# A transformer kernel on one Trainium2 core: the first product behind the turned features waits per eighth, with fewer warm-up products

## The chip, the core and the metric

The kernel runs on one core of one Trainium2 chip. The metric is device time in microseconds of one execution, from the first to the last instruction with what lies around them; the number for a kernel is the median of its runs. All data are float32. Engines are named as in the profile: PE is TensorE (its matmuls; PEld are its weight loads), DVE is VectorE, ACT is ScalarE, POOL is GpSimd, SP is SyncE, which issues the DMAs.

## The reference

Two blocks of two layers each work on 256 tokens of 1024 features. The change lies in the first block. Cut to what matters:

```python
for l in range(DEPTH):                                   # 2 layers
    shift1, scale1, gate1, shift2, scale2, gate2 = split(cond @ w_ada[l] + b_ada[l])
    h = x * (1 + scale1) + shift1
    y = token_mixer(h, w_in[l], ...)                     # p = h @ w_in; attention, spatial gating, gates
    x = layer_norm(ALPHA * x + gate1 * y, ...)
    h = x * (1 + scale2) + shift2
    y = moe_ffn(h, router_w[l], ...)                     # scores = sigmoid(h @ router_w); 64 experts, top 8
    x = layer_norm(ALPHA * x + gate2 * y, ...)
```

So each mixer and each expert layer begins in the same way: x, which lies with the tokens on the partitions, is turned so that features lie on the partitions, is modulated by scale and shift (one pair for each feature, so one for each partition once x is turned), and is then multiplied by a weight matrix: w_in in the mixer, router_w in the expert layer. The second block (attention, a recurrent mixer, two MLPs) is not touched.

## The kernel before

All five engines run one long program each, written out by hand, with semaphores between them. An engine's steps run in program order. `at[...]` holds for each named step the semaphore and the count at which it is done; `reach(pe, ...)` (L329) makes TensorE wait for one, unless it has already waited for as much of the same semaphore. VectorE's steps all count up one semaphore, ScalarE's another.

**The turning.** `turned_pe` (L561) turns x in two halves of 128 tokens (t = 0, 1). Each half is eight transposes of 128x128 (L578), into four PSUM banks; bank k2 holds the eighths 2*k2 and 2*k2 + 1, an eighth being 128 features by 256 tokens. The first half is turned as soon as the layer norm has written it, the second when its turn comes. Around the halves `keep_warm` (L301, products recorded under L304) issues products of the identity whose result nobody reads; they fill TensorE's idle time. After the second half there are six of them (L582), except in the mixer of layer 0, where six stand after the sums of the modulations instead (L944). In the profile each float32 product is two records, so six products are 12.

**The modulation.** `turned_out` (L584) writes the eighths from PSUM into SBUF with scale and shift, one instruction for each eighth. VectorE takes 0, 1, 4 and 5 (recorded under L171), ScalarE takes 2, 3, 6 and 7 (L145). They run beside the warm-up products.

**The wait.** `turned_done` (L594) makes TensorE wait for the last eighth of each engine, 5 and 7, so for all eight. It stands before the first product in `mixer_pe` (L945) and in `moe_pe` (L1499). A `group` (L225) is eight products, one for each eighth, summed in one PSUM bank in the order 0 to 7.

**What follows in a mixer.** `mixer_pe` (L946) multiplies by 15 tiles of w_in, two groups to a tile. Tiles 0 to 6 give two groups of 128 tokens each (i is the tile, t the token half); VectorE copies the results of tiles 0 to 2 out, ScalarE those of 3 to 6. Between them TensorE sums up partial modulations of later steps (`sums_of_partial_pe`, L368, recorded under L376 and L381) that VectorE has formed from pieces of w_ada (`partial_dve`, L356, recorded under L171 and L166). w_in and w_ada come through one DMA queue of SyncE, `mixer_sp` (L904), in turn one tile of w_in and two pieces of w_ada; a transfer into a tile is issued when its former content has been used. VectorE goes on to the rope of queries and keys once the modulations up to tile 7 are made (L1089). POOL loads the mixer's tables at its start (`mixer_pool`, L885).

**What follows in an expert layer.** `moe_pe` (L1497) forms the scores of the router: two groups of eight products, 128 tokens each, 64 columns wide (L1503). Then come the gate product of the shared expert and three warm-up products (L1520). The rest waits for the routing, which VectorE makes (`moe_dve`, L1799). On VectorE the order is: the eighths, then the low part of x less its rounded copy (L1806, recorded under L162), for which ScalarE must have made that copy, and only then the first step on the scores (L1814, recorded under L162 too). On ScalarE (`moe_act`, L1723) the order is: its eighths, the rounded copy of the first half (L1731), the sigmoid of the scores (L1733), the copy of the second half. With the routing of the first four experts made, TensorE gathers their tokens (`gather`, L1552, recorded under L229).

Of the kernel before, what the change touches and what calls it, by code (L numbers as in the profile page):

```python
# [224 lines left out]
def group(pe, out, pairs, start=True, stop=True):  # L225

    ins = None
    for i, (a, b) in enumerate(pairs):
        ins = pe.matmul(out, a, b, start=start and i == 0, stop=stop and i == len(pairs) - 1)  # L229
    return ins  # L230

def program(nc, D, out):
    ctx = ExitStack()
    with ctx:
# [3 lines left out]
        at = Values()  # L239
# [33 lines left out]
        made = signal("pe_made")  # L273
# [27 lines left out]
        def keep_warm(pe, b, n):  # L301

            for _ in range(n):
                pe.matmul(b[:, 0:256], ident[:, :], condr[:, 0:256], start=True, stop=True)  # L304
# [24 lines left out]
        def reach(pe, sem, n):  # L329

            if reached.get(sem, 0) < n:
                pe.wait_ge(sem, n)
                reached[sem] = n
# [227 lines left out]
        def turned_pe(pe, l, which, ready):  # L561

            xk = XS[:, :].rearrange("p (t d k) -> p t k d", t=2, k=8)
            for k2 in range(4):
                _, old = psum.take(("turned", l, which, k2), ("turned out", l, which, 2 * k2 + 1))
                freed(pe, old)
            if l or which:
                keep_warm(pe, psum.of["turned", l, which, 0], 7 if which else 14)
                spare, old = psum.take(("turned warm", l, which))
                freed(pe, old)  # L570
            for t in range(2):
                if t and (l or which):
                    keep_warm(pe, spare, 2 if which else 5)
                reach(pe, *at[ready(t)])
                for k2 in range(4):
                    for kk in range(2):
                        c = kk * 256 + t * 128
                        ins = pe.transpose(psum.of["turned", l, which, k2][:, c:c + 128], xk[:, t, 2 * k2 + kk, :], ident[:, :])  # L578
                    if t:
                        ins.then_inc(*made(("turned", l, which, k2)))  # L580
            if l or which:
                keep_warm(pe, spare, 6)  # L582

        def turned_out(eng, do, mine, dst, l, which):  # L584
            o = l * 32 + which * 16
# [5 lines left out]
                do.fma(dst[:, k * 256:k * 256 + 256], psum.of["turned", l, which, k // 2][:, k % 2 * 256:k % 2 * 256 + 256],  # L591
                       mod1[:, o + 8 + k:o + 9 + k], mod1[:, o + k:o + k + 1], ("turned out", l, which, k))

        def turned_done(eng, l, which):  # L594
            eng.wait_ge(*at["turned out", l, which, 5])
            eng.wait_ge(*at["turned out", l, which, 7])

        LN = [small[:, 16:40].rearrange("p (t s c) -> p t s c", t=2, s=2), small[:, 48:52].rearrange("p (t c) -> p t c", t=2),
              small[:, 52:54]]
# [276 lines left out]
        M = MixerMemory()  # L876
# [49 lines left out]
        def mixer_pe(pe, pump, l):  # L926
            reach(pe, *at["ident"])
            if l == 0:
                reach(pe, *at["cond rows"])
                b, old = psum.take("warm", "cond rows")  # L930
# [5 lines left out]
            if l == 0:  # L936
                sums_of_partial_pe(pe, 0)
                for n in range(4 * FROM[0] - 2, 4 * FROM[0]):
                    reach(pe, *at["mod piece", n])
                    keep_warm(pe, b, 4)  # L940
                sums_of_partial_pe(pe, 1)
                b, old = psum.take("warm behind")
                freed(pe, old)
                keep_warm(pe, b, 6)  # L944
            turned_done(pe, l, 0)  # L945
            for i in range(7):  # L946
                w = weights.of["w_in", l, i].rearrange("p (k c) -> p k c", k=8)
                reach(pe, *at["w_in", l, i])
                for t in range(2):
                    b, old = psum.take(("pz", l, i, t), ("pz out", l, i, t))  # L950
                    freed(pe, old)
                    group(pe, b[:, 0:256], [(M.hv[:, k, t * 128:t * 128 + 128], w[:, k, :]) for k in range(8)]) \
                        .then_inc(*made(("pz", l, i, t)))
                    if t == 0:
                        for u in vector_at(l, i):
                            sums_of_partial_pe(pe, u)
            for i in range(7, 15):
                w = weights.of["w_in", l, i].rearrange("p (k c) -> p k c", k=8)
                reach(pe, *at["w_in", l, i])
                for c in range(2):  # L960
                    b, old = psum.take(("gates", l, i, c), ("gates out", l, i, c))
# [7 lines left out]
            for a in range(3):  # L969
                b, old = psum.take(("qkT", l, a), ("qkT out", l, a))  # L970
                freed(pe, old)
                for s in range(2):
                    for t in range(2):
# [4 lines left out]
                        ins = pe.transpose(b[:, s * 256 + t * 128:s * 256 + t * 128 + 128], src, ident[:, :])  # L978
# [7 lines left out]
            for gg in range(2):  # L986
                b, old = psum.take(("sgu", l, gg), ("sgu out", l, gg))
                freed(pe, old)
                for g in range(4 * gg, 4 * gg + 4):
                    o = g % 4 * 128  # L990
                    ins = pe.matmul(b[:, o:o + 128].rearrange("p (t d) -> p t d", t=2), M.wsv[:, g, :],
                                    M.Zv[:, :, 512 + g * 64:576 + g * 64], start=True, stop=True)
# [184 lines left out]
        E = ExpertMemory()  # L1177
# [318 lines left out]

        def moe_pe(pe, l):  # L1497
            turned_pe(pe, l, 1, lambda t: ("ln", ("mixer", l), t))
            turned_done(pe, l, 1)  # L1499
            reach(pe, *at["router", l])  # L1500
            b, old = psum.hold(ACC, ("scores", l), ("scores out", l))
            freed(pe, old)
            for t in range(2):  # L1503
                ins = group(pe, b[:, t * 64:t * 64 + 64],
                            [(E.hv[:, k, t * 128:t * 128 + 128], E.rv[:, k, :]) for k in range(8)])
            ins.then_inc(*made(("scores", l)))
            def shared_half(name):
                b, w = psum.of[name, l], weights.of["ws_" + name[7:], l].rearrange("p (k f) -> p k f", k=8)
                reach(pe, *at["ws_" + name[7:], l])
# [2732 lines left out]
```

## Time and profile before

| | |
|---|---|
| median of 3 runs | 2992.61 us (2990.23 to 2993.92) |
| profiled execution, its own time | 2994.28 us |
| its span, first to last instruction | 2992.5 us |
| mean granted TensorE clock | 0.984 |
| PE busy | 2798.5 us, 94% of the span |
| DVE busy | 1629.0 us, 54% |
| ACT busy | 756.6 us, 25% |
| HBM traffic | 239 GB/s over the span |
| the two mixers of the first block begin to turn at | 21.5 us and 805.8 us |
| the two expert layers begin to turn at | 259.5 us and 1023.1 us |

Times in the profile count from the span's start. The profiled execution took 1.78 us more than its span. A timeline row reads: start, duration, engine, line, operation, names written<-read, shape, number of instructions merged in it, and in brackets the idle time of the engine ahead of it with what ended it. A row of stretches reads: the stretch, its length, for each engine its busy time and instructions, the granted TensorE clock as a share of full speed, the busy share of the 16 DMA engines, and GB/s. A row of grouped instructions ends with busy time, mean ns of one, and idle time ahead of them.

### The profile page before, as it was taken

The page shows a single profiled execution, that of the slowest core. Times are in us where ns is not written, and L with a number is a line of the kernel's source. Part 1 is how long each engine was busy: PE and PEld are TensorE (multiplying, and loading weights), DVE is VectorE, ACT ScalarE, POOL GpSimd, SP SyncE. Part 2 cuts the span into 40 slices and gives each one's busy share as a digit, 9 for nine tenths or more (in the row PEclk, how much of TensorE's full clock was granted, in tenths as well). Part 3 has the DMA queues.
Part 4 walks back from the last instruction along what each step waited for, and adds up shares of the span by engine and source line. Part 5 has one row for each costly group of instructions (what it writes and reads, how often), then busy time and mean ns, then how long its engine had stood idle before and what let it go on. Part 6 is the DMA issues. An engine that isn't in the chain of part 4 may idle for free.

```text
span 2992.5 us, 65346 instructions
## 1 busy us (share of the span) xinstructions
PE 2798.5 (94%) x27418; PEld 2077.7 (69%) x27418; DVE 1629.0 (54%) x2821; ACT 756.6 (25%) x1400; POOL 409.8 (14%) x343
## 2 busy tenths in 40 slices
PE   7999999988899999999989899999998999899998
PEld 6878566655587866655557588844577887888973
DVE  6745433333473554444436478788757536555555
ACT  0122212121112133323213422200045414443210
POOL 1000000000000000000000036400014302434630
PEclk9999999999999999999999999999999999999999
DMA  9945999999984599999974035485430023000443
GB/s 392 389 161 219 406 405 415 386 421 420 389 365 141 205 381 420 419 407 420 420 310 141 15 113 171 168 308 197 154 106 18 4 82 129 18 16 33 157 167 112
DMA packets 102704, 718.31 MB, mean 240 GB/s; under 512 B 11680, under 2 KB 11968, under 8 KB 18176
## 3 DMA queue, kind: packets, MB, share of 16 engines
q1 hardware_dynamic: 98448, 700.02, 59.5%
q0 software_dynamic: 3952, 14.00, 1.5%
q8 instruction: 220, 3.60, 0.5%
q14 instruction: 84, 0.69, 0.1%
HBM read 711.09 MB, written 2.88 MB: 239 GB/s over the span
## 4 chain that ended last, share of the span: by engine, by line
PE 74%; DVE 12%; DMA 9%; ACT 2%; issue 2%; SPq 0%; POOL 0%; DVEq 0%; ACTq 0%; POOLq 0%
PE ps L229 16%; PE ps L1614 10%; PE ps L2167 9%; PE ps L2192 7%; DMA arena<-in_w_up 6%; DVE arena L162 6%; PE ps L3139 5%; PE ps L1643 5%; PE ps L2832 3%; PE ps L1705 2%; ACT arena L145 2%; DMA arena<-in_w_down 2%; DVE arena L166 2%; PE ps L2559 1%; PE ps L3571 1%
## 5 line engine op out<-in xcount | busy, mean ns | idle before, releaser
L145 ACT ACTIVATE arena<-ps 128x512 f32<-128x512 f32 (+3 forms) x529 | 266.9, 505 | 1268.0 <-PE ps L229 244.7
L229 PE MATMUL ps<-arena 128*128 128x256 f32 x2144 | 480.1, 385 | 18.5 <-DMA arena<-in_w_in 4.9
L162 POOL TENSOR_TENSOR arena<-arena 128x512 f32<-128x512 f32 (+1 forms) x288 | 376.4, 1307 | 821.7 <-DVE arena L162 284.4
L229 PEld LDWEIGHTS ps<-arena 128*128 128x128 f32 x2144 | 408.7, 192 | 87.1 <-issue 9.7
L1614 PE MATMUL ps<-arena 128*32 128x256 f32 (+2 forms) x5120 | 390.8, 389 | 42.0 <-DMA arena<-in_w_up 31.0
L1614 PEld LDWEIGHTS ps<-arena 128*32 128x32 f32 (+2 forms) x5120 | 248.5, 120 | 187.4 <-issue 87.8
L162 DVE TENSOR_TENSOR arena<-ps,arena 128x256 f32<-128x256 f32 (+3 forms) x416 | 203.8, 490 | 235.0 <-PE ps L3139 87.9
L162 DVE TENSOR_TENSOR arena<-arena 128x512 f32<-128x512 f32 (+6 forms) x473 | 294.1, 622 | 60.7 <-PE ps L2192 35.7
L2167 PE MATMUL ps<-arena 128*128 128x256 f32 (+1 forms) x1792 | 298.5, 328 | 2.2 <-DVE arena L162 1.5
L2192 PE MATMUL ps<-arena 128*128 128x512 f32 x672 | 293.0, 593 | 2.4 <-DVE arena L162 2.2
L2167 PEld LDWEIGHTS ps<-arena 128*128 128x128 f32 x1792 | 270.0, 191 | 29.6 <-DVE arena L171 3.3
L166 DVE SCALAR_TENSOR_TENSOR arena<-arena,cond 128x1024 f32<-128x1024 f32 x154 | 230.5, 1497 | 26.5 <-DMA arena<-in_w_ada 18.4
L2192 PEld LDWEIGHTS ps<-arena 128*128 128x128 f32 x672 | 125.8, 190 | 155.9 <-issue 136.8
L3139 PE MATMUL ps<-arena 64*64 64x64 f32 x7168 | 200.1, 220 | 26.7 <-DVE arena L162 18.3
L162 DVE TENSOR_TENSOR arena<-arena,ps 128x256 f32<-128x256 f32 (+3 forms) x177 | 83.3, 471 | 248.2 <-ACT arena L145 121.8
L3139 PEld LDWEIGHTS ps<-arena 64*64 64x64 f32 x7168 | 182.3, 134 | 45.1 <-DVE arena L162 23.3
L1643 PE MATMUL ps<-arena 128*32 128x512 f32 (+2 forms) x1280 | 192.9, 607 | 15.9 <-DMA arena<-in_w_down 12.6
L166 DVE SCALAR_TENSOR_TENSOR arena<-ps,arena,gates 128x512 f32<-128x512 f32 x104 | 78.1, 751 | 215.9 <-PE ps L1643 215.9
L1643 PEld LDWEIGHTS ps<-arena 128*32 128x32 f32 (+2 forms) x1280 | 56.9, 119 | 121.0 <-issue 118.5
L145 ACT ACTIVATE rounded<-arena 128x512 fp32r<-128x512 f32 x104 | 65.6, 630 | 293.0 <-DVE arena L166 293.0
L1705 PE MATMUL ps<-rounded 128*128 128x512 f32 x416 | 122.5, 419 | 12.6 <-issue 4.9
L186 DVE COPY arena<-ps 128x256 f32<-128x256 f32 (+2 forms) x128 | 67.7, 529 | 114.9 <-PE ps L978 46.2
(278 smaller groups left out, 2912.1 us busy)
## 6 DMA issues: line engine op xcount, KB each, us to landing
arena<-in_w_gate SPq DMA_DIRECT2D x128, 1024.0 KB, 13.0
arena<-in_w_up SPq DMA_DIRECT2D x128, 1024.0 KB, 14.1
arena<-in_w_down SPq DMA_DIRECT2D x128, 1024.0 KB, 13.5
arena<-in_mlp SPq DMA_DIRECT2D x80, 1024.0 KB, 4.8
arena<-in_w_ada SPq DMA_DIRECT2D x48, 1024.0 KB, 13.1
arena<-in_ada SPq DMA_DIRECT2D x48, 1024.0 KB, 4.9
arena<-in_w_in SPq DMA_DIRECT2D x30, 1024.0 KB, 11.3
arena<-in_w_rkv SPq DMA_DIRECT2D x20, 1024.0 KB, 4.9
```

Of the source, the lines that this page charges most:

```text
L145: self.e.activation(out, in_, func, bias=bias, scale=scale, **more).then_inc(*self.done(key))
L162: self.e.tensor_tensor(out, a, b, op).then_inc(*self.done(key))
L166: self.e.scalar_tensor_tensor(out, a, s, b, op0, op1).then_inc(*self.done(key))
L186: self.e.tensor_copy(out, a).then_inc(*self.done(key))
L229: ins = pe.matmul(out, a, b, start=start and i == 0, stop=stop and i == len(pairs) - 1)
L1614: ins = pe.matmul(psum.of["gu", l, new][o:o_, i_ * 256:i_ * 256 + 256], xe[:, k, new % 2 * 128 + o:new % 2 * 128 + o_], w[i_].rearrange("p ...
L1643: ins = pe.matmul(bb[o:o_, :], E.HTT[:, j * 128 + o:j * 128 + o_], w[:, j, nh * 512:nh * 512 + 512], start=j == 0, stop=j == 1)
L1705: ins = pe.matmul(psum.tiles[ACC + t * 2 + nh][:, :], E.ST[p % 2][:, t * 128:t * 128 + 128], y_[:, nh * 512:nh * 512 + 512], start=p == 0 ...
L2167: ins = pe.matmul(psum.of["p", l, i, p][:, 0:m.n], hidden_left(l, i, p, j), m.moving(p, j), start=j == 0, stop=j == 3)
L2192: ins = pe.matmul(psum.of["p", l, "out", s, p][:, :], a, b, start=j == 0, stop=j == 15)
L2832: ins = pe.matmul(b[:, c * 256:c * 256 + 256], w[:, k, c * 128:c * 128 + 128], src[:, k, :], start=k == 0, stop=k == 7)
L3139: yield pe.matmul(b[other(o) if cross else o, a, :], lhs[o, a, :], rhs[o, a, :], start=start and a == 0, stop=stop and a == 7)
```

## The change

It has two parts, at all four places (the mixer and the expert layer of each of the two layers):

- Of the six warm-up products that stand behind the second half of the turning (in the mixer of layer 0: behind the sums of the modulations) one is left.
- The wait for all eight eighths is gone. The first group of products (the first 128 tokens, with the first tile of w_in or with the router) waits ahead of each product for that product's eighth alone, and takes the eighths in the order 0, 2, 1, 3, 4, 6, 5, 7, so by turns one that VectorE made and one that ScalarE made. The second group stands behind it in the old order.

```diff
@@ turned_pe
             if l or which:
-                keep_warm(pe, spare, 6)
+                keep_warm(pe, spare, 1)
@@
-        def turned_done(eng, l, which):
-            eng.wait_ge(*at["turned out", l, which, 5])
-            eng.wait_ge(*at["turned out", l, which, 7])
+        def first_product(pe, l, which, out, pairs_of):
+
+            for n, k in enumerate((0, 2, 1, 3, 4, 6, 5, 7)):
+                reach(pe, *at["turned out", l, which, k])
+                ins = pe.matmul(out, *pairs_of(k), start=n == 0, stop=n == 7)
+            return ins
@@ mixer_pe
                 sums_of_partial_pe(pe, 1)
                 b, old = psum.take("warm behind")
                 freed(pe, old)
-                keep_warm(pe, b, 6)
-            turned_done(pe, l, 0)
+                keep_warm(pe, b, 1)
             for i in range(7):
...
-                    group(pe, b[:, 0:256], [(M.hv[:, k, t * 128:t * 128 + 128], w[:, k, :]) for k in range(8)]) \
-                        .then_inc(*made(("pz", l, i, t)))
+                    if i or t:
+                        ins = group(pe, b[:, 0:256], [(M.hv[:, k, t * 128:t * 128 + 128], w[:, k, :]) for k in range(8)])
+                    else:
+                        ins = first_product(pe, l, 0, b[:, 0:256], lambda k: (M.hv[:, k, 0:128], w[:, k, :]))
+                    ins.then_inc(*made(("pz", l, i, t)))
@@ moe_pe
             turned_pe(pe, l, 1, lambda t: ("ln", ("mixer", l), t))
-            turned_done(pe, l, 1)
...
-            for t in range(2):
-                ins = group(pe, b[:, t * 64:t * 64 + 64],
-                            [(E.hv[:, k, t * 128:t * 128 + 128], E.rv[:, k, :]) for k in range(8)])
-            ins.then_inc(*made(("scores", l)))
+            first_product(pe, l, 1, b[:, 0:64], lambda k: (E.hv[:, k, 0:128], E.rv[:, k, :]))
+            group(pe, b[:, 64:128], [(E.hv[:, k, 128:256], E.rv[:, k, :]) for k in range(8)]) \
+                .then_inc(*made(("scores", l)))
```

## Rows read from the trace of the kernel before

**Rows 1.** The page: the chain that ended last, by engine and by line.
```profile
PE 74%; DVE 12%; DMA 9%; ACT 2%; issue 2%; SPq 0%; POOL 0%; DVEq 0%; ACTq 0%; POOLq 0%
PE ps L229 16%; PE ps L1614 10%; PE ps L2167 9%; PE ps L2192 7%; DMA arena<-in_w_up 6%; DVE arena L162 6%; PE ps L3139 5%; PE ps L1643 5%; PE ps L2832 3%; PE ps L1705 2%; ACT arena L145 2%; DMA arena<-in_w_down 2%; DVE arena L166 2%; PE ps L2559 1%; PE ps L3571 1%
```

**Rows 2.** The timeline, head of the mixer of layer 0.
```profile
33.84 4.52 PE L304 MATMUL ps<-condr,ident 128*128 128x256 f32 x12
...
34.27 2.42 ACT L145 ACTIVATE arena<-ps,mod 128x256 f32<-128x256 f32 x4 [30.90 <-DVE mod L166]
34.29 2.35 DVE L171 TENSOR_SCALAR arena<-ps,mod 128x256 f32<-128x256 f32 x4
...
38.20 13.98 PE L229 MATMUL ps<-arena 128*128 128x256 f32 x64
...
53.48 7.17 PE L229 MATMUL ps<-arena 128*128 128x256 f32 x32 [1.30 <-DMA arena<-in_w_in]
...
64.27 5.41 PE L229 MATMUL ps<-arena 128*128 128x256 f32 x16 [3.61 <-DMA arena<-in_w_in]
```

**Rows 3.** Busy time by stretch: head of the mixer in layer 0 and in layer 1.
```profile
34.28:37.70 3.42, 3.42 (x10) 2.71 (x9) 3.05 (x6) 3.18 (x5) 0.71 (x2) 0.50 1.01 392
...
812.00:820.00 8.00, 8.00 (x38) 7.03 (x38) 5.45 (x6) 1.49 (x2) 3.02 (x6) 1.00 0.99 237
```

**Rows 4.** The timeline, VectorE ahead of the rope in the mixer of layer 0.
```profile
96.99 5.32 DVE L166 SCALAR_TENSOR_TENSOR arena<-arena,cond 128x1024 f32<-128x1024 f32 x4 [2.50 <-DMA arena<-in_w_ada]
...
102.52 0.17 DVE L166 SCALAR_TENSOR_TENSOR mod<-ps,vecs 128x8 f32<-128x8 f32 x1 [0.21 <-PE ps L381]
```

**Rows 5.** The timeline, head of the mixer of layer 1.
```profile
809.57 2.35 DVE L171 TENSOR_SCALAR arena<-ps,mod 128x256 f32<-128x256 f32 x4 [0.75 <-PE ps L578]
...
809.78 2.42 ACT L145 ACTIVATE arena<-ps,mod 128x256 f32<-128x256 f32 x4 [6.96 <-PE ps L578]
809.86 2.76 PE L304 MATMUL ps<-condr,ident 128*128 128x256 f32 x12
...
812.46 17.86 PE L229 MATMUL ps<-arena 128*128 128x256 f32 x82
```

**Rows 6.** Grouped instructions of TensorE from 812.4 to 867.9 us.
```profile
L229 PE MATMUL ps<-arena 128*128 128x256 f32 x240 | 52.4, 379 | 0.0
```

**Rows 7.** The page: the costliest groups, weight loads of the group helper.
```profile
L229 PEld LDWEIGHTS ps<-arena 128*128 128x128 f32 x2144 | 408.7, 192 | 87.1 <-issue 9.7
```

**Rows 8.** The timeline, mixer of layer 1 ahead of and behind the rope.
```profile
862.69 5.31 DVE L166 SCALAR_TENSOR_TENSOR arena<-arena,cond 128x1024 f32<-128x1024 f32 x4 [2.35 <-DMA arena<-in_w_ada]
...
869.64 0.17 DVE L166 SCALAR_TENSOR_TENSOR mod<-ps,vecs 128x8 f32<-128x8 f32 x1 [1.63 <-PE ps L381]
...
886.73 3.50 PE L229 MATMUL ps<-arena 128*128 128x256 f32 x15 [1.50 <-ACT arena L145]
```

**Rows 9.** The timeline, head of the expert layer of layer 0.
```profile
262.48 2.76 PE L304 MATMUL ps<-condr,ident 128*128 128x256 f32 x12
...
263.08 2.42 ACT L145 ACTIVATE arena<-ps,mod 128x256 f32<-128x256 f32 x4
...
265.59 2.07 ACT L145 ACTIVATE rounded<-XS 128x1024 fp32r<-128x1024 f32 x1
265.60 3.76 PE L229 MATMUL ps<-routing,arena 128*128 128x64 f32 x32 [0.37 <-issue]
267.69 2.03 DVE L162 TENSOR_TENSOR rounded<-XS,rounded 128x1024 fp32r<-128x1024 f32 x1 [3.16 <-ACT rounded L145]
...
269.39 0.28 ACT L145 ACTIVATE arena<-ps 128x128 f32<-128x128 f32 x1 [1.73 <-PE ps L229]
...
269.86 0.29 DVE L162 TENSOR_TENSOR arena<-arena,routing 128x128 f32<-128x128 f32 x1
```

**Rows 10.** The timeline, the gather of layer 0 and of layer 1.
```profile
281.36 4.07 PE L229 MATMUL ps<-rounded 128*128 128x256 f32 x32 [1.69 <-DVE rounded L162]
...
1044.91 5.45 PE L229 MATMUL ps<-rounded 128*128 128x256 f32 x32 [1.67 <-DVE rounded L162]
```

## The prediction

> **What bounds the kernel now.** I read the chain that ended last first: TensorE carries 74% of it, VectorE 12%, DMA 9% [rows 1]. So a change on TensorE can pay, but only in a stretch where the chain runs through TensorE. The change touches four short stretches: the head of each of the two mixers and of each of the two expert layers. I read each of them in the timeline, always for the same thing: what comes last behind the edited place. Where a fifth view, the busy time by stretch, matters, it is for the granted clock and the DMA share.
>
> **Mixer of layer 0.** The six warm-up products take 4.52 us from 33.84, because the clock is granted at 0.50 (the 1.2 GHz level of the two) from 34.28 to 37.70 [rows 2, 3]. Behind them come 64 product records, then TensorE idles 1.30 us and 3.61 us for w_in from memory [rows 2]; the DMA engines are fully busy there, with a share of 1.01 [rows 3]. Starting earlier only makes these two waits longer. What counts is the place where the branch leaves for VectorE: the modulation step at 102.52 waited 0.21 us for TensorE, and VectorE's own sums of w_ada had ended at 96.99 + 5.32 = 102.31, held by DMA [rows 4]. So this edit can give 0.2 us at most, however early TensorE is. I take 0.2, with bounds 0 and 0.21.
>
> **Mixer of layer 1.** This is the one place where the edit lies on the path. Before, 12 records of warm-up (two to a product) run from 809.86 for 2.76 us, and the first real product starts at 812.46, directly behind them; the old wait for all eighths costs nothing beyond that [rows 5]. VectorE makes eighths 0, 1, 4, 5 from 809.57 at 2.35 / 4 = 0.59 us each, so they end near 810.11, 810.70, 811.34 and 811.92; ScalarE makes 2, 3, 6, 7 from 809.78 at 0.60 us, ending near 810.35, 810.95, 811.60 and 812.20 [rows 5]. A record takes 17.86 / 82 = 0.218 us, a product 0.44 us [rows 5]. With one warm-up product TensorE is free at 809.86 + 0.44 = 810.30. In the new order 0, 2, 1, 3, 4, 6, 5, 7 the products start at 810.30, 810.74, 811.17, 811.61, 812.05, 812.48, 812.92 and 813.35. Each eighth is there at least 0.2 us before its product, even the last one by over 1 us. So no new wait takes any time, and the stream of products starts 812.46 - 810.30 = 2.16 us earlier: ten records less.
>
> The eight waits themselves stand on TensorE's queue, and everything behind them (the second token half, the other w_in tiles, the sums for the modulations) is queued behind. I price a wait that is already met at 0: from 812.4 to 867.9 TensorE issues 240 such records, with waits for weights, banks and sums among them, and its idle time is 0.0 [rows 6]. The upper bound is one exposed weight load for each of eight products, 8 x 0.192 = 1.5 us [rows 7]. 
>
> Does 2.16 us last? TensorE has no idle time up to 867.9 [rows 6], so its part ends 2.16 us earlier. But at 869.64 VectorE's modulation step had waited only 1.63 us for TensorE: its own sums had ended at 862.69 + 5.31 = 868.00, and these were waiting for w_ada [rows 8]. That transfer does not come earlier. SyncE issues w_in and w_ada as TensorE frees tiles, so it will issue up to 2.16 us sooner, but from 812 to 820 the engines are already at a share of 0.99 with the tables of the POOL queue [rows 3]. So 1.63 us is what is left; the bounds are 2.16 (the stream moves up too) and 0.6 (exposed weight loads). VectorE's rope and the norm follow, then ScalarE's sigmoids that free banks, for which TensorE waits 1.50 us at 886.73 [rows 8]. That wait grows a little, and the 1.63 us passes on to the end of the kernel, because the later loads are released by TensorE's own progress.
>
> **Both expert layers.** In layer 0 the warm-up starts at 262.48, and the router's 32 records at 265.60, 0.12 us behind ScalarE's last eighth (263.08 + 2.42 = 265.50) [rows 9]. They take 3.76 / 32 = 0.118 us each. After the change only the last product, 2 records, waits for the last eighth; 14 of the first 16 are done by 265.60, so the scores come 14 x 0.118 = 1.6 us earlier. But VectorE, which turns scores into routing, works in program order: it first subtracts the rounded copy (267.69 to 269.72), which waits for ScalarE's copy (265.59 to 267.66), and its first step on the scores follows at 269.86, 0.14 us behind its own last step [rows 9]. The sigmoid at 269.39 moves up to about 267.8, and VectorE is late next instead. I take 0 for each layer; layer 1 shows the same rows. Bounds: 0, and 1.6 us if the order on VectorE did not hold.
>
> What moves is TensorE's idle time. The shared gate product and the three warm-up products behind it end 1.6 us earlier, while the routing does not, so TensorE rests longer before the gather. The gather took 4.07 us in layer 0 and 5.45 us in layer 1, after nearly the same idle time (1.69 and 1.67 us) [rows 10]; in layer 1 part of it ran at the low clock. So one fall of the clock here costs 5.45 - 4.07 = 1.38 us. The Trainium skill (TensorE: Matmul & The Clock Gate, "HAM oscillation — how this bites in real kernels") says that a wait between bursts of products lets the array fall back to the low clock, so that the next burst starts cold. By that rule both gathers start cold, and the sum gets 1.38 us worse. The two rows agree with it in one layer and not in the other, so I take half of it, +0.7 us, with bounds -1.38 (layer 1 recovers) and +2.76 (both layers lose one more).
>
> **Sum.** -0.2 - 1.63 + 0 + 0.7 = -1.1 us. The profiled execution took 2994.28 us (span 2992.5), which would become 2993.2; it lies 1.7 us above the median of the runs, 2992.61, so I predict 2992.61 - 1.1 = 2991.5 us. About 0.2% (6 us) is what a measurement of this kernel can tell from no change, so the forecast is "same".
>
> **Rivals.**
> - Everything counts (the DMA stream follows, and VectorE takes the scores when they come): -2.16 - 0.2 - 2 x 1.6 = -5.6, 2987.0 us. For it: TensorE's large share of the chain. Against: the program order on VectorE [rows 9]. Chance 0.08.
> - Nothing moves: the gain in mixer 1 is eaten by exposed weight loads or by the later DMA waits, or the waits do not let a product go before all eighths are done. Then the 0.6 us or less drowns, 2992.6 us. Chance 0.17.
> - Slower, by the clock. Place: the gather of each expert layer. Price: a gather wholly at half the clock takes 2 x 4.07 = 8.14 us, 4.07 more in layer 0 and 8.14 - 5.45 = 2.69 more in layer 1, 6.8 us; less 1.8 us from the mixers this is 2997.6 us. It decides when the gather's first record starts at a granted 0.50 and the whole gather stays there. For it: removed warm-up work and longer rests. Against: the row of layer 1, where a gather that began low did recover [rows 10]. Chance 0.1; with the further steps behind the gather at the low clock too it passes 0.2% in about half of these.
>
> **How the numbers follow.** The forecast (gain in mixer 1, nothing from the experts, a clock term of either sign) has 0.65. Its own ends are 2992.61 - 2.16 - 0.21 - 1.38 = 2988.9 and 2992.61 + 2.76 - 0.6 = 2994.8. The three runs shown differ by 3.7 us, from 2990.23 to 2993.92, so I widen this by under 1 us on either side: 2988.0 to 2995.5, which holds the second rival and leaves out the first and most of the third, under 0.2. Faster by over 0.2%: 0.06; slower by over 0.2%: 0.06, both from the tails of the first and third rival and from what I have overlooked; within: 0.88.
>
> **What would show it.** Right: in mixer 1 the first products directly behind two warm-up records and under way by about 810.3 on this clock; the modulation step near 868.1 waiting for w_ada, no longer for TensorE; in the expert layers the scores early and VectorE's first step on them where it was, 0.1 us behind the subtraction; in mixer 0 longer waits for w_in. Wrong: idle time between the products of the first group; the first step on the scores well under 4.4 us after ScalarE's last eighth; or gathers of 8 us.

## The result, and the profile after

The changed kernel takes 2997.18 us (median of 20 runs, 2991.45 to 3004.89), the kernel before beside it 2992.3 us (20 runs, 2984.59 to 2998.49). The ratio is 1.0019 with a 95% interval of 1.001 to 1.0028. So the change makes the kernel some 5 to 6 us slower, where 1.1 us less was forecast; the time lies outside the range given.

The profiled execution of the changed kernel took 2999.37 us (span 2997.6, mean granted clock 0.980, before 0.984). Its chain of waits has hardly changed: TensorE 73%, DMA 10% against the 74% and 9% of [rows 1]. The change has to be read at its four places.

**Expert layer of layer 0**, the timeline:

```profile
263.79 0.60 PE L304 MATMUL ps<-condr,ident 128*128 128x256 f32 x2
264.22 0.37 PE L598 MATMUL ps<-routing,arena 128*128 128x64 f32 x2
265.01 2.29 PE L598 MATMUL ps<-routing,arena 128*128 128x64 f32 x14 [0.42 <-ACT arena L145]
266.91 2.08 ACT L145 ACTIVATE rounded<-XS 128x1024 fp32r<-128x1024 f32 x1
267.14 2.60 PE L229 MATMUL ps<-routing,arena 128*128 128x64 f32 x16
269.02 2.04 DVE L162 TENSOR_TENSOR rounded<-XS,rounded 128x1024 fp32r<-128x1024 f32 x1 [3.18 <-ACT rounded L145]
269.53 8.19 PE L229 MATMUL ps<-arena 128*128 128x256 f32 x32
269.77 0.28 ACT L145 ACTIVATE arena<-ps 128x128 f32<-128x128 f32 x1 [0.78 <-PE ps L229]
271.20 0.29 DVE L162 TENSOR_TENSOR arena<-arena,routing 128x128 f32<-128x128 f32 x1
282.60 6.77 PE L229 MATMUL ps<-rounded 128*128 128x256 f32 x32 [1.59 <-DVE rounded L162]
```

Against [rows 9]: the router's first record stands 2.69 us ahead of ScalarE's copy of the features (266.91; both began together before), but the first 16 are paced by the eighths, and the second 16 take 2.60 us, 0.16 us each in place of 0.118. The first step on the scores (271.20) still stands directly behind VectorE's subtraction (269.02 + 2.04 = 271.06). The shared gate takes 8.19 us, and the gather 6.77 in place of the 4.07 us of [rows 10]. Busy time by stretch, three stretches of layer 0 and three of layer 1 (router, shared gate, gather):

```profile
264.20:269.50 5.30, 4.88 (x33) 4.45 (x33) 1.98 (x4) 4.44 (x6) 0.00 (x0) 0.88 0.93 380
269.50:277.70 8.20, 8.20 (x35) 7.10 (x35) 7.38 (x22) 3.63 (x3) 0.00 (x0) 0.87 1.02 424
282.60:289.30 6.70, 6.70 (x33) 6.57 (x33) 2.98 (x9) 2.21 (x4) 0.00 (x0) 0.54 0.37 149
1031.00:1036.40 5.40, 5.39 (x33) 5.40 (x34) 2.08 (x1) 2.90 (x3) 0.00 (x0) 0.67 0.99 296
1036.40:1045.10 8.70, 8.70 (x34) 7.36 (x34) 7.41 (x26) 3.65 (x4) 0.00 (x0) 0.81 1.02 429
1048.20:1052.30 4.10, 4.10 (x33) 3.97 (x33) 2.97 (x9) 2.43 (x5) 0.00 (x0) 1.00 1.02 412
```

The granted clock falls to its lower level for a part of the router and of the shared gate in both layers. In the profile of the kernel before, all four of these stretches stand at 1.00 (router and shared gate of layer 0, then of layer 1):

```profile
265.60:269.40 3.80, 3.80 (x33) 3.80 (x34) 1.71 (x1) 2.07 (x2) 0.00 (x0) 1.00 1.02 423
269.40:276.30 6.90, 6.90 (x33) 6.07 (x33) 6.08 (x22) 3.63 (x3) 0.00 (x0) 1.00 1.01 421
1029.30:1033.00 3.70, 3.70 (x33) 3.70 (x34) 1.65 (x1) 2.02 (x1) 0.00 (x0) 1.00 1.00 242
1033.00:1040.00 7.00, 7.00 (x34) 6.17 (x33) 6.18 (x22) 3.64 (x3) 0.00 (x0) 1.00 1.01 422
```

**Expert layer of layer 1**, the same timeline:

```profile
1028.52 2.35 DVE L171 TENSOR_SCALAR arena<-ps,mod 128x256 f32<-128x256 f32 x4 [0.75 <-PE ps L578]
1031.01 1.98 PE L598 MATMUL ps<-routing,arena 128*128 128x64 f32 x16 [1.60 <-DVE arena L171]
1032.82 3.60 PE L229 MATMUL ps<-routing,arena 128*128 128x64 f32 x16
1036.21 8.84 PE L229 MATMUL ps<-arena 128*128 128x256 f32 x32
1036.76 0.29 DVE L162 TENSOR_TENSOR arena<-arena,routing 128x128 f32<-128x128 f32 x1 [0.63 <-ACT arena L145]
```

Here no product waits for an eighth of its own. TensorE rests 1.60 us, until VectorE has written its last eighth (1028.52 + 2.35 = 1030.87): the bank of the scores (`ACC`, bank 4) still holds a turned eighth in this layer. Then the second 16 records take 3.60 us, 0.225 each, and the scores come too late for VectorE by 0.63 us.

**Mixer of layer 1**, TensorE at the head and VectorE at the modulation step:

```profile
815.85 0.60 PE L304 MATMUL ps<-condr,ident 128*128 128x256 f32 x2
816.29 3.65 PE L598 MATMUL ps<-arena 128*128 128x256 f32 x16
819.77 20.45 PE L229 MATMUL ps<-arena 128*128 128x256 f32 x94
...
868.14 5.31 DVE L166 SCALAR_TENSOR_TENSOR arena<-arena,cond 128x1024 f32<-128x1024 f32 x4 [2.27 <-DMA arena<-in_w_ada]
873.57 0.17 DVE L166 SCALAR_TENSOR_TENSOR mod<-ps,vecs 128x8 f32<-128x8 f32 x1
```

This is as forecast: two warm-up records, the products right behind them without idle time, and a modulation step that no longer waits for TensorE (1.63 us in [rows 8]).

**Mixer of layer 0**, the last w_in products before the modulations, and the modulation step:

```profile
64.30 6.66 PE L229 MATMUL ps<-arena 128*128 128x256 f32 x16 [3.77 <-DMA arena<-in_w_in]
...
103.80 0.17 DVE L166 SCALAR_TENSOR_TENSOR mod<-ps,vecs 128x8 f32<-128x8 f32 x1 [1.77 <-PE ps L381]
```

The 16 records took 5.41 us before [rows 2], at a granted 0.68, and take 6.66 here, at 0.55; the step at 103.80 stands 1.28 us later than before. Whether the change did that is one question for the runs.

How the profiled 5.1 us come together, by how much later VectorE's n-th instruction starts than before (both lists have 2821): +1.3 up to the first expert layer, +2.6 in its head, +2.1 in its rounds, -2.05 in mixer 1, -1.3 in the rest of that mixer's layer, -0.8 in the head of the second expert layer, +3.2 from there to the end. The +2.6 falls in the gather: up to its start VectorE has lost 0.0 us in this head, although router and shared gate ran slowly. In the second head it has lost 0.6 us at that point, and the gather, faster here than before (4.09 for 5.45 us), gives back 1.4. This is one execution against one other, and the experiments say which of it belongs to the change.

### The profile page after: what moved, and what is told of

Same layout as the page of the kernel before. It is cut to its first block, busy times and chain, and to the rows that moved or that the text cites. A ratio compares the mean times of both kernels' runs of the same rounds, so it can differ in the third digit from the quotient of the medians.

```text
span 2997.6 us, 65259 instructions
## 1 busy us (share of the span) xinstructions
PE 2799.8 (93%) x27378; PEld 2074.3 (69%) x27378; DVE 1629.0 (54%) x2821; ACT 756.7 (25%) x1400; POOL 409.7 (14%) x343
## 4 chain that ended last, share of the span: by engine, by line
PE 73%; DVE 12%; DMA 10%; ACT 2%; issue 2%; SPq 0%; POOL 0%; DVEq 0%; ACTq 0%; POOLq 0%
PE ps L229 16%; PE ps L1617 10%; PE ps L2170 9%; PE ps L2195 7%; DMA arena<-in_w_up 6%; DVE arena L162 6%; PE ps L3142 5%; PE ps L1646 5%; PE ps L2835 3%; PE ps L1708 2%; ACT arena L145 2%; DVE arena L166 2%; DMA arena<-in_w_down 2%; PE ps L2562 1%; DMA arena<-in_w_ada 1%
```

## The experiments

Theory A: the products taken out of the expert layers let the granted clock fall in the router and the shared gate there, and this costs more than mixer 1 gives back. Rivals: B, the waits by eighths break the stream on TensorE; C, a delay at the head of an expert layer is taken up again by the waits for weights in the rounds behind it; D, the mixers' part costs time too. All ratios are to the kernel before on the same chip. The mean clock is that of a kernel's runs, beside 0.9832 to 0.9842 for the kernel before in the four sets.

### One part alone: the mixers

```diff
-                keep_warm(pe, spare, 6)
+                keep_warm(pe, spare, 6 if which else 1)
```

The mixers as in the change, the expert layers as before.

> The change in the two mixers alone; the expert layers as before. Theory (the loss sits in the expert layers, where TensorE falls to half clock): 2 us faster than before, ratio 0.9993, with the first product of mixer 1 ten records earlier and the gathers as before (4 to 5.5 us). Rival 1 (the mixer of layer 0 loses its clock in the longer waits for w_in and hands the delay on): 3 to 6 us slower, ratio 1.001 to 1.002. Rival 2 (the waits ahead of each product cost time on TensorE's queue): no gain in mixer 1, ratio 1.000 or above.

Measured: 0.9999 (0.9986 to 1.0011), clock 0.9847. The mixers show no cost: the 1.001 to 1.002 that D asks for lie at the end of the interval or above it. The 0.9993 of the theory lies inside it too, so a gain in the whole time is not shown either. VectorE gained 2.1 us in mixer 1, and in mixer 0 it stood 0.2 us later than before. The gather of layer 0 happened to run at the low clock, with router and shared gate as before (3.76 and 7.12 us):

```profile
281.61 6.76 PE L229 MATMUL ps<-rounded 128*128 128x256 f32 x32 [1.68 <-DVE rounded L162]
```

So a gather of 6.8 us, which the changed kernel's profile shows too, needs none of the expert layers' edits.

### One part alone: the expert layers

```diff
-                keep_warm(pe, spare, 6)
+                keep_warm(pe, spare, 1 if which else 6)
-            turned_done(pe, l, 1)
+            first_product(pe, l, 1, b[:, 0:64], lambda k: (E.hv[:, k, 0:128], E.rv[:, k, :]))
```

> The change in the two expert layers alone; the mixers as before. Theory: 7 us slower than before, ratio 1.0023, with router, shared gate or gather of each layer partly at a granted clock of 0.50; gather up to 6.8 us instead of 4.1. Rival 1 (mixer 0): no difference, ratio 1.000. Rival 3 (the difference only arises in the expert rounds by chance): no difference from before in the heads, ratio within 0.1% of 1.

Measured: 1.0007 (0.9997 to 1.0017), clock 0.9817. That is less than the 1.0023 expected. The medians of these runs, 2999.16 and 2994.57 us, are 1.0015 apart, so the ratio may be somewhat low; the repetition below gave 1.0018. The timeline of layer 0:

```profile
264.35 2.29 PE L598 MATMUL ps<-routing,arena 128*128 128x64 f32 x14 [0.42 <-ACT arena L145]
266.48 3.12 PE L229 MATMUL ps<-routing,arena 128*128 128x64 f32 x16
269.39 9.33 PE L229 MATMUL ps<-arena 128*128 128x256 f32 x32
281.96 4.08 PE L229 MATMUL ps<-rounded 128*128 128x256 f32 x32 [0.26 <-DVE rounded L162]
```

The low clock lies in the router's second half and in the shared gate (9.33 us for the 7.12 of the kernels with six). It eats the rest ahead of the gather, 0.26 us left of 1.69 [rows 10], and in this layer VectorE is not later at the gather than the kernel before. So in this layer the rest covers what the low clock costs in router and shared gate. In layer 1 of this profile the clock held (3.75 and 7.13 us).

### The warm-up products alone

The expert layers wait for all eighths as before and in the old order, but have one warm-up product in place of six; the mixers as before.

```diff
-                keep_warm(pe, spare, 6)
+                keep_warm(pe, spare, 1 if which else 6)
```

> Only the expert layers: one warm-up product in place of six, but the wait for all eight eighths and the old order kept. Theory (what hurts is the missing work on TensorE, not the waits): as slow as the change in the expert layers alone, ratio 1.002, with the router, shared gate or gather partly at 0.50. Rival 2 (the waits ahead of each product): no difference from before, ratio 1.000.

Measured: 1.0031 (1.0019 to 1.0043), clock 0.9802, the slowest of all, and slower than the 1.002 expected. The timeline of layer 0:

```profile
263.25 7.06 PE L229 MATMUL ps<-routing,arena 128*128 128x64 f32 x32 [2.52 <-issue]
270.10 8.59 PE L229 MATMUL ps<-arena 128*128 128x256 f32 x32
...
270.65 0.29 DVE L162 TENSOR_TENSOR arena<-arena,routing 128x128 f32<-128x128 f32 x1 [3.14 <-ACT arena L145]
```

TensorE rests 2.52 us where the five products were, and the whole router then runs at the lower level: 7.06 us for 3.76 in [rows 9]. Here the scores come so late that VectorE waits 3.14 us for them (2.38 us in layer 1), and it is later by the start of the gather by 3.15 us in layer 0 and 3.1 in layer 1. Of the delay in layer 0 all but 0.2 us is still there where the second expert layer begins. A rule of the Trainium skill (TensorE: Matmul & The Clock Gate, "HAM oscillation — how this bites in real kernels") says that a wait between bursts of products lets the array fall back, so that the next burst starts cold; this pair of rows, 2.52 us of rest and then a router at a granted 0.50, agrees with it. Shorter rests went both ways: behind 1.60 us ahead of the router of layer 1, the clock fell in both profiles of the change and held in both of its expert half.

### The waits alone

The expert layers wait by eighths, as in the change, with the six warm-up products kept; the mixers as before.

```diff
-            turned_done(pe, l, 1)
+            first_product(pe, l, 1, b[:, 0:64], lambda k: (E.hv[:, k, 0:128], E.rv[:, k, :]))
```

> Only the waits of the two expert layers are changed (one eighth at a time); all six warm-up products stay in all four places. Theory A (the warm-up products taken out of the expert layers let the granted clock fall in the router and the shared gate): router 3.8 us and shared gate 7.1 us at a granted 1.00 in both layers, mean clock of the runs 0.983 to 0.985, time within 1.5 us of the kernel before, ratio 0.9995 to 1.0005. Rival B (the waits themselves break the stream of products on TensorE): router over 5 us in at least one layer, idle time between its records, ratio 1.0007 or more.

Measured: 0.9995 (0.9983 to 1.0007), clock 0.9832. The timeline of layer 0:

```profile
262.28 1.89 PE L598 MATMUL ps<-routing,arena 128*128 128x64 f32 x16
264.01 1.95 PE L229 MATMUL ps<-routing,arena 128*128 128x64 f32 x16
265.80 7.12 PE L229 MATMUL ps<-arena 128*128 128x256 f32 x32
266.00 0.28 ACT L145 ACTIVATE arena<-ps 128x128 f32<-128x128 f32 x1 [1.12 <-PE ps L229]
267.07 0.29 DVE L162 TENSOR_TENSOR arena<-arena,routing 128x128 f32<-128x128 f32 x1
278.49 5.59 PE L229 MATMUL ps<-rounded 128*128 128x256 f32 x32 [1.60 <-DVE rounded L162]
```

The eight products that wait by eighths, 16 records, take 1.89 us, 0.118 us a record, exactly as without such waits [rows 9], and no idle time stands ahead of them. So B falls. The scores leave ScalarE at 266.28 and VectorE takes them at 267.07, directly behind its subtraction: the waits bring nothing either, as the prediction said of VectorE's order.

With the runs before, this makes a square for the expert layers: six products and all eighths 1, six and by eighths 0.9995, one and all eighths 1.0031, one and by eighths 1.0007 (and 1.0018 in the repetition below). The cost comes with the products taken out. With all eighths the whole interval lies above 1. By eighths the two repetitions, 1.0013 on average, lie 0.0018 above the 0.9995 with six products, which is only just clear of the noise. The waits by eighths give a part of the cost back, 1.0031 against 1.0013. The rows show where this can come from: behind the start of the one warm-up product the router begins after 0.44 us in layer 0 and 2.20 us in layer 1 of the expert half, and after 3.12 us in both where it waits for all eighths.

### Work put back ahead of the gather

Three kernels with four more products on TensorE's rest ahead of each gather: the whole change with them, the mixers' part with them, and the kernel before with them.

```diff
                 freed(pe, old)
+                if Q == 0 and k == 0:
+                    keep_warm(pe, b, 4)
                 reach(pe, *at["seated", l, Q])
```

> The whole change, and four more warm-up products (into the bank that the gather overwrites) just ahead of the wait for the first gather. Theory: both gathers at the full clock, 4.1 us, so at most the router and the shared gate still run slowly, which VectorE's order hides in part; 1 to 3 us faster than before, ratio 0.9993, and 6 us or more faster than the change alone. Rival 1 and rival 2: no better than the change alone, ratio 1.0015 to 1.002.

> The mixers as in the change, the heads of the expert layers as before (all eighths waited for, six warm-up products), and four more warm-up products on TensorE's idle time ahead of each gather. Theory A: gathers of about 4.1 us at a granted 1.00 in both layers, idle time ahead of them under 0.3 us, the gain of mixer 1 kept (about 2 us), on the whole 3 to 6 us less than before, ratio 0.998 to 0.999. Rival C (what the head of an expert layer loses or gains is taken up again by waits for weights in the rounds): ratio 0.9993, the 2 us of mixer 1 alone.

> The kernel before with four more warm-up products on TensorE's idle time ahead of each gather. Theory A: both gathers 4.1 us at a granted 1.00, 1.4 us less in the layer where the gather was at the low clock, 1 to 3 us in all, ratio 0.999 to 0.9997. Rival C: 1.000. If the four products end later than what the gather waits for, the gather starts up to 0.4 us late and part of it is lost.

Measured: the whole change with them 1.0006 (0.9994 to 1.0018), the mixers' part 0.9988 (0.9976 to 1.0000), the kernel before 0.9989 (0.9977 to 1.0001). The timeline of layer 0 in the mixers' part:

```profile
278.18 1.89 PE L304 MATMUL ps<-condr,ident 128*128 128x256 f32 x8
279.94 4.09 PE L229 MATMUL ps<-rounded 128*128 128x256 f32 x32
```

All six gathers of the three kernels take 4.09 to 4.18 us at a granted 1.00. For the whole change 6 us or more against the change alone had been expected; 1.0006 against 1.0019 is 4 us, and the two intervals overlap. In the whole change the router of layer 1 still took 5.97 us, at a clock of 0.60: the fill cures the gather and not the router, and the kernel stays on the slow side. In the other two, with six products at the head, router and shared gate stand at 3.76 and 7.1 us. The kernel before with the fill also answers for mixer 0, which it leaves untouched:

```profile
65.06 6.13 PE L229 MATMUL ps<-arena 128*128 128x256 f32 x16 [4.62 <-DMA arena<-in_w_in]
...
104.03 0.17 DVE L166 SCALAR_TENSOR_TENSOR mod<-ps,vecs 128x8 f32<-128x8 f32 x1 [0.48 <-PE ps L381]
```

The step stands 1.5 us later than in the profile before, as it does in the changed kernel (1.28). Over all profiles it stands later by 0.6 us on average in the seven with the mixers' edit (0.0 to 1.5) and by 0.6 in the six others without it (0.1 to 1.5). So such a delay comes and goes between executions, and no part of it can be put down to the change.

### What a delay at this place costs

The kernel before with sixteen products in place of six in the expert layers: later, but with TensorE busy.

```diff
-                keep_warm(pe, spare, 6)
+                keep_warm(pe, spare, 16 if which else 6)
```

> The kernel before with sixteen warm-up products in place of six at the head of each expert layer, so that the router starts 10 x 0.436 = 4.4 us later in each layer with TensorE busy all the while and the clock untouched. It measures what a delay at the head of an expert layer costs by the end. Theory A (such a delay is handed on): 2 x 4.4 = 8.7 us, ratio 1.0025 to 1.003. Rival C (it is taken up again by waits for weights in the rounds): under 3 us, ratio below 1.001.

Measured: 1.0013 (1.0002 to 1.0025), clock 0.9852, the highest of all. Both heads run at full clock (3.68, 7.13 and 4.07 us in layer 0), and VectorE waits for the scores in layer 0:

```profile
273.60 0.29 DVE L162 TENSOR_TENSOR arena<-arena,routing 128x128 f32<-128x128 f32 x1 [3.71 <-ACT arena L145]
```

The 8.7 us of A would be 1.0029, above the interval; 1.0013 is 3.9 us, with an interval from 0.6 to 7.5 us. But VectorE did not get the 4.4 us: by its own instructions it is 3.6 us later in each head, some 7 us in both. Whether the rounds take up a part of that or hand on all of it, this run does not tell; both fit.

### Everything by eighths, with the work put back

The whole change, with six products kept in the expert layers and five more ahead of the gather.

```diff
-                keep_warm(pe, spare, 1)
+                keep_warm(pe, spare, 6 if which else 1)
+                if Q == 0 and k == 0:
+                    keep_warm(pe, b, 5)
```

> The whole change, but with six warm-up products kept in the expert layers, and five more ahead of each gather. Theory A: router 3.7 us, shared gate 7.1 us and gather 4.1 us, all at a granted 1.00 in both layers, mean clock 0.984 to 0.986, ratio 0.998 to 0.9995: with the TensorE work put back the same waits are no longer slower than before. The eighths bring nothing by themselves (VectorE's order), so the same as the variant with all eighths waited for in the expert layers, within 0.1%. Rival B (the waits by eighths cost time of their own): 1.001 or more.

Measured: 0.9997 (0.9985 to 1.001), clock 0.9834. Router 3.68, shared gate 7.13 and gather 4.2 us, all at 1.00, in both layers. The gather begins right behind the fifth product, and head by head (from the router's first record to the gather's last) it takes 20.5 us against 19.76 in the variant that waits for all eighths. Of these 0.7 us, 0.5 are the router's earlier start, and the other 0.2 may be the fifth product's. So the same waits show no cost here, and no gain.

### The mixers with fill again, and the change again

> The same kernel as the one with the mixers changed, the expert heads as before and four products ahead of each gather, measured once more against the kernel before to narrow its interval. Theory A: 0.998 to 0.9992, below 1 with its whole interval when both measurements are taken together. Rival C: 0.9993 to 1.0005.

> The changed kernel itself once more, beside its expert half alone, on one chip. Open is whether the 1.0019 of the change and the 1.0007 of its expert half belong together. Theory A (cost in the expert layers by the clock, a gain of about 2 us in mixer 1): the mean clock 0.981 to 0.983, below that of the kernel before; ratio 1.0003 to 1.0018; the whole change 1 to 3 us faster than its expert half alone. Rival D (the mixers' part costs time too, by the clock in mixer 0): the whole change as slow as its expert half or slower.

> The expert half of the change alone once more, on the same chip as the whole change. Theory A: ratio 1.0008 to 1.0022, router or shared gate at a granted clock under 1.00 in at least one layer, mean clock 0.981 to 0.983. Rival C (the rounds take the delay up): 0.9995 to 1.0005.

Measured: the mixers' part with the fill 0.9992 (0.9979 to 1.0004), with the first time on average 0.999, and by the two intervals about 0.9981 to 0.9999. So it is faster than the kernel before, by some 3 us. The kernel before with the fill alone (0.9989) cannot be told from it, so what the mixers' part adds is not shown. The change again 1.001 (0.9996 to 1.0023), and its expert half on the same chip 1.0018 (1.0004 to 1.0032), clocks 0.9831 and 0.9823. The whole change is 3.7 us faster than its expert half by the medians (2993.56 and 2997.23 us) and 2.4 by the ratios, where 1 to 3 were expected of mixer 1; the ratios of the first measurements stood the other way round (1.0019 and 1.0007), and the intervals hold a difference of nothing. In the change's second profile the clock kept up in layer 0's router, and one sees what the eighths alone do to the products when only one warm-up product stands ahead:

```profile
261.46 2.29 PE L598 MATMUL ps<-routing,arena 128*128 128x64 f32 x14 [0.43 <-ACT arena L145]
263.58 1.95 PE L229 MATMUL ps<-routing,arena 128*128 128x64 f32 x16
279.02 5.95 PE L229 MATMUL ps<-rounded 128*128 128x256 f32 x32 [0.93 <-DVE rounded L162]
```

Fourteen records take 2.29 us in place of 1.65 (14 x 0.118), with 0.43 us of rest ahead: TensorE runs into the eighths as they are written. So the 4.87 us of this router are at full clock. In layer 1 the router took 5.52 us at a clock of 0.65.

### The heads side by side

| kernel | layer 0: router, shared gate, gather (us) | layer 1 | ratio |
|---|---|---|---|
| before | 3.76, 7.13, 4.07 | 3.76, 7.12, 5.45 | 1 |
| mixers only | 3.76, 7.12, 6.76 | 3.76, 7.12, 4.10 | 0.9999 |
| experts by eighths, six products | 3.68, 7.12, 5.59 | 3.68, 7.12, 6.59 | 0.9995 |
| mixers, fill | 3.76, 7.13, 4.09 | 3.76, 7.12, 4.10 | 0.9988 |
| before, fill | 3.76, 7.13, 4.10 | 3.76, 7.13, 4.10 | 0.9989 |
| the change | 5.51, 8.19, 6.77 | 5.40, 8.84, 4.09 | 1.0019 |
| the change again | 4.87, 7.13, 5.95 | 5.52, 8.72, 4.08 | 1.0010 |
| experts only | 6.03, 9.33, 4.08 | 3.75, 7.13, 5.58 | 1.0007 |
| experts only again | 6.04, 9.33, 4.10 | 3.75, 7.13, 5.59 | 1.0018 |
| the change, fill | 4.87, 7.13, 4.17 | 5.97, 8.25, 4.18 | 1.0006 |
| one product, all eighths | 7.06, 8.59, 4.07 | 6.25, 9.65, 4.09 | 1.0031 |

With six or more products ahead, router and shared gate ran at a granted 1.00 in all 16 heads of eight profiles (three of them are not in the table: sixteen products, all by eighths with fill, and the mixers with fill again). With one product the clock fell in 8 of 12. The gather, in kernels without a fill, falls in either group: 4.07, 5.45, 6.76 and 4.10 us in the kernel before and the mixers' part, mean 5.1; 6.77, 4.09, 5.95 and 4.08 in the change, mean 5.2. Where the low clock in router and shared gate left TensorE a rest of 0.12 to 0.50 us ahead of the gather, in six heads, the gather kept the full clock (4.07 to 4.10 us).

## Why the prediction was wrong, step by step

**Mixer of layer 0 (-0.2 us).** The size stands: nothing to gain. A delay like that in the profile of the changed kernel stands in a kernel without the edit as well.

**Mixer of layer 1 (-1.63 us).** Right in mechanism up to the modulation step. In the changed kernel's profile VectorE gains 2.05 us, over the seven profiles with this edit 2.05, 2.12, 2.12, 1.83, 1.3, 1.3 and 0.86, mean 1.65; in the profiles without it 0.0. What varies is the transfer of w_ada, of which the prediction said that it "does not come earlier". The wait for TensorE shrank from 1.63 to 0.12 us, and the sums' end moved by 873.45 - 868.00 = 5.45 us while VectorE came in 5.98 late, so w_ada came 0.53 us earlier: 1.51 + 0.53 = 2.04. In the change's second profile it came 0.66 us later, 1.51 - 0.66 = 0.85. The price of 0 for the eight waits holds: the 16 records take 3.65 us, which is 16 x 0.218 and the tail of the last one. The rule cited beside it (the Trainium skill, TensorE: Matmul & The Clock Gate; it stands there under "Architectural detail: the array is 16× 32×32, not 1× 128×128", not under the heading that the prediction names) would have cost 1.5 us by the way it was used; no run here shows that.

The last step, that TensorE's wait for ScalarE's sigmoids "grows a little" and the gain "passes on to the end", was too simple. In two of the seven profiles (the change again, and all by eighths with fill) that wait grew from the 1.50 us of [rows 8] to 2.76 and 2.32 us, and the 3.5 us behind it stand at a granted 0.56 and 0.66, where the profile before has 1.00:

```profile
887.02 39.94 PE L229 MATMUL ps<-arena 128*128 128x256 f32 x176 [2.76 <-ACT arena L145]
```

These 176 records take 38.25 us in the twelve other profiles. VectorE lost the 1.69 us that they took longer, and with it the whole gain. In the other five profiles the gain passed this place unchanged, in one of them (the change with fill) behind a rest of 2.35 us at which the clock did not fall.

**The expert layers at 0.** VectorE's order held in layer 0, as forecast: its first step on the scores comes 4.4 us behind ScalarE's last eighth, as before. The scores came 0.94 us earlier and not 1.6, because the second 16 records ran partly at the lower clock; in the change's second profile, where the clock held in this router, they came 1.6 us earlier, as forecast. The rest of 0.42 us between the first records is the idle time that the prediction named as a sign against it. In layer 1 the step "layer 1 shows the same rows" was wrong: the bank of the scores is held by an eighth until 1030.87, and the router starts 2.2 us behind its warm-up product, only 0.9 us less than with all eighths. That could have been read from the kernel before.

**The clock term (+0.7 us). This is the step that failed**, and the sum with it. The prediction moved TensorE's idle time to one place only, behind the shared gate, and looked for the fall of the clock in the gather; it took the router and the shared gate at full speed. The products taken out stood ahead of the router, and the fall came there, in 8 of 12 heads against none of 16, while the gathers were no slower than before. In layer 1 of the change's two profiles the slow router and shared gate even shortened the rest ahead of the gather, from 1.67 to 0.16 and 0.28 us. The course that was forecast is seen in one head, layer 0 of the second profile: the clock held, TensorE rested 1.71 us ahead of the routing's products and 0.93 us ahead of the gather, and the gather took 5.95 us. The runs size the expert half, for which 0.7 us was forecast, at 1.0007 and 1.0018, on average 1.0013 or some 4 us (about 1 to 6 us by the intervals). The slower rival had the right sign and looked to the clock too, but named the wrong place, the gather for its whole length; no gather of 8 us was seen.

**What stays open.** That the products taken out cost the time is shown by the square of runs, and that the clock falls in router and shared gate by the profiles. How a low clock there reaches the end is seen only in the kernel that waits for all eighths, where VectorE is over 3 us later in each head. In the five profiles with one product and waits by eighths (both of the change, both of its expert half, and the change with fill), VectorE has lost 0.0 us at the gather of layer 0 and 0.6, 0.7, 0.0, 0.0 and 1.2 us at that of layer 1. So for the change itself most of the 4 us does not show in the heads, and its way through the clock is argued and not shown. In the expert half's two profiles VectorE falls 3 us behind in the first round, where TensorE waits 2.6 and 2.7 us for w_up and the clock falls behind that rest. But such a rest of 2.5 to 2.75 us also stands in three kernels with six products (the mixers alone, the waits alone, the mixers with fill again), and in one of them the clock fell behind it too. Over all profiles the clock fell at this place in four of six with one product and in two of eight with six or more. An effect of 1 to 2 us at one such place is below what these measurements resolve, and it is left open.

## What to carry to other kernels

Before taking out filler work ahead of a product, ask what clock the next products on that engine will get, all of them up to the next rest, and not only the one that was slow in the trace at hand. A head start on TensorE is worth what the engine behind it can take: here VectorE's program order took none of it in layer 0's expert layer, and in mixer 1 VectorE gained 0.9 to 2.1 us of the 2.16. A head start also makes the next rest longer: in mixer 1 the clock fell behind that rest in two of seven profiles and took the gain back. Fillers put where TensorE rests anyway, as ahead of the gather, kept the clock there in every head. Together with the mixers' part they made a kernel some 3 us faster than the one before; which of the two parts gave it, these runs do not separate.

## What had not been expected of the hardware

The same kernel's time varies with the clock it happens to get. The 35 runs of the kernel before in the first set lie between 2985.97 and 3003.87 us with mean granted clocks from 0.979 to 0.987, and time and clock go together (correlation -0.80, about 1.7 us for each 0.001; 1.9 to 2.2 us in the three other sets). Where in a kernel the clock falls differs from execution to execution; one profile of each kernel shows a change of the clock's places that the edit did not make, such as the gathers here, and only the count over many profiles separated the two. That time and clock go together does not say which of the two leads.
